# Six row places instead of eight, and one gate weight kept on chip for all latent groups

## The reference, cut to what matters

```python
proj = h @ lp['w_in']
u, v, zb, q, k, rv, rg_f, rg_b, gm = jnp.split(proj, IN_OFFSETS, axis=-1)
y_a = _gmlp_mix(jax.nn.gelu(u), jax.nn.gelu(v), lp['gmlp_ws'], lp['gmlp_b'], lp['gmlp_ln_g'])
y_b = _pool_mix(zb, lp['pool_w'], lp['pool_scale'], grid)
...
ga, gb, gc = jnp.split(jax.nn.sigmoid(gm), N_BRANCH, axis=-1)
merged = ga * y_a + gb * y_b + gc * y_c.astype(x.dtype)
x = x + gt1 * (merged @ lp['w_out'])
...
# _peer, per block of 128 tokens
qp = (xt @ wq).reshape(t, PEER_HEADS, 2, PEER_DKEY // 2)
sc = jnp.einsum('thsk,hsnk->thsn', qp, subkeys).astype(jnp.float32)
top_s, top_i = lax.top_k(sc, PEER_TOPK)
...
act = jax.nn.gelu(jnp.einsum('thkd,td->thk', u_tab[expert], xt).astype(jnp.float32))
wgt = (g * act).astype(xt.dtype)
return jnp.einsum('thk,thkd->td', wgt, v_tab[expert]).astype(xt.dtype)
```

## Time and profile before

| | |
|---|---|
| median of three executions | 4546.5 us (4540.7 to 4548.8) |
| the profiled execution | 4553.9 us, its span 4552.2 us |
| PE busy | 3751.7 us (82%), 12065 instructions |
| DVE busy | 2791.9 us (61%) |
| ACT busy | 1640.3 us (36%) |
| POOL busy | 1626.2 us (36%), 1280 gathers |
| DMA | 1671.7 MB, mean 367 GB/s over the span |
| gathers (queue q0) | 1342.3 MB |

### The profile page before, as it was taken

How to read it: one execution, slowest core, us unless ns; L and a number is a source line. 1 busy time by engine, 2 the same in 40 slices (tenths; PEclk the granted TensorE clock), 3 DMA queues, 4 the chain that set the end, 5 groups by cost and what they waited for, 6 DMA issues and landing times. The chain is left out here.

```text
span 4552.2 us, 44585 instructions
## 1 busy us (share of the span) xinstructions
PE 3751.7 (82%) x12065; PEld 1565.1 (34%) x12065; DVE 2791.9 (61%) x6341; ACT 1640.3 (36%) x5133; POOL 1626.2 (36%) x1312
## 2 busy tenths in 40 slices
PE   8999999999998689999776887888777566666666
PEld 6654455656553233443221222342222111111110
DVE  1122777577676976655898557455678984444444
ACT  4211345232113343334344334334344553333333
POOL 0000123223222333333434434343444445555554
PEclk9999999999999799999876999998887666666666
DMA  8646688789999989999998999999999999999998
GB/s 345 235 161 219 261 331 328 274 305 378 372 405 401 364 352 402 383 380 407 402 393 325 421 415 403 397 396 413 403 402 382 395 395 413 413 421 413 415 422 348
DMA packets 277595, 1671.68 MB, mean 367 GB/s; under 512 B 30496, under 2 KB 47968, under 8 KB 90848
## 3 DMA queue, kind: packets, MB, share of 16 engines
q0 software_dynamic: 184320, 1342.26, 73.6%
q1 hardware_dynamic: 84864, 303.14, 17.3%
q10 hardware_dynamic: 8160, 23.43, 1.6%
HBM read 1630.93 MB, written 37.78 MB: 367 GB/s over the span
## 5 line engine op out<-in xcount | busy, mean ns | idle before, releaser
L1103 POOL DMA_INDIRECT slots<-in_peer,idxR x1280 | 1619.9, 1266 | 2854.9 <-PE ps L1417 1793.8
L1417 PE MATMUL ps<-slots,lhs 128*64 128x512 f32 x4544 | 1496.2, 773 | 698.9 <-ACT lhs L1159 684.8
L1707 DVE CUSTOM_DVE_ANT_0 slots<-slots,h2R 128x1024 f32<-128x1024 f32 x1280 | 1547.3, 1224 | 756.5 <-issue 694.8
L1399 PE MATMUL ps<-ring,arena 128*128 128x512 f32 (+1 forms) x3264 | 1368.8, 576 | 15.4 <-ACT arena L1349 6.9
L1417 PEld LDWEIGHTS ps<-slots,lhs 128*64 128x64 f32 x4544 | 296.8, 159 | 1792.0 <-ACT lhs L1159 1537.7
L1399 PEld LDWEIGHTS ps<-ring,arena 128*128 128x128 f32 x3264 | 624.0, 195 | 771.7 <-issue 754.3
L1148 ACT ACTIVATE gelus<-dots 128x1 f32<-128x1 f32 x1280 | 256.4, 200 | 1511.4 <-DVE dots L1707 1499.6
L1159 ACT ACTIVATE lhs<-fold,wgts 128x64 f32<-128x64 f32 x1136 | 395.1, 348 | 37.2
L1151 ACT ACTIVATE wgts<-gelus,gsmR 128x1 f32<-128x1 f32 x1280 | 377.1, 295 | 42.4 <-ACT gelus L1148 0.5
L1399 PE MATMUL ps<-ring,slots 128*128 128x512 f32 (+1 forms) x576 | 223.3, 548 | 0.0
L1719 DVE SCALAR_TENSOR_TENSOR slots<-slots,wgts 128x1024 f32<-128x1024 f32 x135 | 173.0, 1282 | 79.0 <-ACT wgts L1151 73.0
(11 more groups left out here) (206 smaller groups left out, 2407.0 us busy)
## 6 DMA issues: line engine op xcount, KB each, us to landing
ring<-in_whead SPq DMA_DIRECT2D x48, 1024.0 KB
ring<-in_wa SPq DMA_DIRECT2D x48, 1024.0 KB
ring<-in_wq SPq DMA_DIRECT2D x32, 1024.0 KB
slots<-in_peer,idxR POOLq DMA_INDIRECT x1280
ring<-in_wgc SPq DMA_DIRECT2D x16, 1024.0 KB
ring<-in_wgb SPq DMA_DIRECT2D x16, 1024.0 KB
ring<-in_wout SPq DMA_DIRECT2D x16, 1024.0 KB
o_scratch<-inb SPq DMA_DIRECT2D x80, 128.0 KB
```

Source lines behind the costliest of these rows:

```text
L1103: g.indirect_dma_start(out=slot(R), out_offset=None, in_=a["peer"], in_offset=bass.IndirectOffsetOnAxis(ap=idxR[:, p % KEEP, g2, col:col + ...
L1399: done = mm(out, lhsT, rhs, start=n == 0, stop=n == KD - 1)
L1417: done = mm(ps[j * HALF:(j + 1) * HALF, g2, :], weights, slot(R)[:, D + j * UW:D + (j + 1) * UW], start=start, stop=stop)
L1707: v.tensor_tensor_reduce(out=u, in0=u, in1=h2R[:, g2, :], scale=1.0, scalar=0.0, op0=ALU.mult, op1=ALU.add, accum_out=dots[:, R % LHS:R % ...
```

## The change

`SLOTS` falls from 8 to 6, so every row uses six places and `displaced(R)` is R - 6 throughout; `slots` keeps its size of eight places (`PLACES`). Places 6 and 7 become `kept`, a home for the first unit of the pooled branch's gate. SP loads it once in the latent stage, behind a wait for group 0's indices (`idx_done`), by when the scores in these places have been read. For groups 1 to 3 the gate's tiles of j = 0 read `kept` and belong to no unit, so the ring no longer loads that unit for them. Group 0 loads it into the ring as before.

```diff
-SLOTS = 8
+SLOTS = 6
+PLACES = 8
...
-                ev = self.add("gb", 1, ("wgb", j, k), g=k, i=i, j=j, c=cs[i], p=BASE[k] + i, pe=7.0, act=.7, dve=1.5)
+                ev = self.add("gb", 1, ("wgb", j, k) if j or not k else None, g=k, i=i, j=j, c=cs[i], p=BASE[k] + i, pe=7.0, act=.7, dve=1.5)
...
-        slots = sb("slots", [P, SLOTS, 2 * D])
+        slots = sb("slots", [P, PLACES, 2 * D])
...
+        kept = slots[:, SLOTS:PLACES, :].rearrange("p s n -> p (s n)")
...
                 elif k == "z" and ev.i == 0:
+                    if ev.g and ev.j:
+                        sp.wait_ge(s["idx_done"], 8 * BASE[1])
+                        sp.dma_start(kept, a["wgb"][0]).then_inc(s["kept_in"], 16)
...
-                    if ends and n == KD // 2 - 1 and tile == last[ev.u]:
+                    if ends and n == KD // 2 - 1 and tile == last.get(ev.u):
...
                     room(t)
+                    if k == "gb" and ev.j == 0 and ev.g:
+                        pe.wait_ge(s["kept_in"], 16)
+                        w = kept.rearrange("p (k n) -> p k n", k=KD)
```

More of the change, by code:

```diff
@@ L793, in build @@
         modd = nc.dram_tensor("mod_scratch", [8, D], F32, kind="Internal").ap()
-        names = """const_in silu_done cond_in bmod_in pool_consts decay_in lg_exp lg_u lg_ln lg_done exps_done mask_done
+        names = """const_in silu_done cond_in bmod_in kept_in pool_consts decay_in lg_exp lg_u lg_ln lg_done exps_done mask_done
             m8_out m8_in mod_done pk_done modd_out lng_in subk_in psc_in pw_in hT_out hg_in state_in state_out
```

## The result

The changed kernel takes 4694.1 us (median of four, 4692.9 to 4701.6) against 4544.8 us before: the ratio is 1.0323, 95% interval 1.0311 to 1.0335. It is 149 us slower. The sign was forecast and the wide range, 4532 to 4730, holds the time, but the forecast's own range, 4556 to 4670, does not: the forecast was +65 us, and the loss is more than twice that.

The account below looks back on a forecast made before the run. The bound varies by stretch: TensorE, VectorE while ranking, DMA when full, with the row-place loop as a second budget. Losses of 75 us less 10 gained, +65 on 4546.5, gave 4610 us; own range 4556 to 4670, wide range 4532 to 4730.

Parts of the forecast that it names:

- The tail: From 3700 us on, only rows are left and DMA sets the pace; 5 us lost for pauses at a chunk's end.
- G: Time from POOL's gather instruction to the row's dot product; 7.76 us with a short queue, 12.7 beside weight loads.
- H: Time from a row's dot product to POOL's next instruction for its place; 9.75 us in the dense stretch, 5.05 at the end.
- The stretch from 1300 to 2200: TensorE and DMA both nearly full; six places were to lose 20 us, between 0 and 46.
- The dense stretch: From 2500 to 3500 us, DMA full at 0.99; six places were to lose 35 us, a third of 101.
- midway value: Dense stretch with G = 10.2 us: a row takes 3.33 us, a loss of 101 us.
- The upper end of G: Dense stretch, three gathers sharing DMA with weight loads: G = 12.7 us, a row takes 3.74, a loss of 238 us.
- rival C: Idle TensorE lowers its own clock, from 0.90 towards 0.80 in the dense stretch: +130 to +200 us, chance 0.22.
- 2200 to 2500: VectorE's expert ranking is the bound, as in 3500 to 3700; 10 us lost for both, 0 to 42.
- A: Faster: the gather queue never runs dry with six places and the saved loads count in full; 4532 to 4537 us, chance 0.18.
- B: Nothing measurable: a small loss of 10 to 20 us equals the gain; 4537 to 4556 us, chance 0.12.
- D: SP stalls on its new wait or the kept load comes late, at group 1's gate; 4550 to 4600 us, chance 0.02.

Follow-up runs that it names:

- the pair with few weight bytes: Weight transfers of groups 2 and 3 cut from 1 MB to 128 KB, in the kernel before with eight places and with six: 4492.5 and 4643.0 us.

## Why the prediction was right or wrong

**Right.** The sign, the bytes, the order, and the absence of a cost for SP's wait, TensorE's wait and the kept load (six places alone gave 1.0330, the change 1.0323). The tail: G fell from 15.3 to 9.9 with H at 5 and 2.49 us a row, +4 us where I said 5. The 500 to 800 stretch, six places in both, did not move. The stretch from 1300 to 2200 lost 22 us where I said 20, but partly by luck: VectorE's waits for gathers grew by 63 us there (83 to 146), not by 40, and a third of that reached the time, not half.

**Wrong, by terms.**
- The dense stretch, "a third of 101: 35 us", measured 89, and this is the step that failed. I let H "shrink towards 5.05" when TensorE waits, and so struck out two thirds of the midway value. H did not shrink: over rows 547 to 882 its mean is 8.1 us before and 7.9 after, while G fell from 15.8 to 11.6 (the i-th gather and the i-th dot of the timelines). A place is held while TensorE is in a tile, as the earlier trace rows show with H = 9.75 and a silence of POOL of 7 us. (G + H)/N with measured means is the time of a row whatever the cause, 19.4/6 = 3.24 us, so it explains nothing by itself; the forecast hung on what H and G would become. The upper end of G, weight loads beside the gathers, was the wrong mechanism (the pair with few weight bytes lost the same 150). The midway value without the third, 101, would have been nearer.
- The sum also left the clock at nothing and kept it for rival C; 43 of the 89 us are longer busy time of TensorE at 0.86 instead of 0.90.
- 2200 to 2500: +20, and 3500 to 3700: -1; I had 10 for both together. The loss of the first is in group 2's queries and ranking, the place in its order that answers to the scene above; that its cause is the same was not tested. By rows, 405 to 517 lose 23 us.
- 800 to 1300: +13, I had 5 (upper end 21), and I gave "within 5 us of itself" as a sign. VectorE's waits for gathers grew from 1 to 47 us there.
- The gain, 10 us, measured 4 (1 slower to 8 faster) with eight places.

By stretches, 89 + 22 + 13 + 19 + 4 = 147 net, where the sum had 75 less the gain of 10.

**The rivals.** A (the queue never runs dry) is out: DMA went from 0.99 to 0.93. B is out by the time. Of C, the clock did fall, from 0.90 to 0.86 in the dense stretch, but not below the 0.85 that I gave as its sign, and TensorE's idle share there rose by 3 points, from 18% to 21%, where C supposed 5. C's time, 4680 to 4750, is the one that came, a clock part and a loop part together. Whether the slower clock caused a part of the loss, or filled time in which rows were late anyway, was not tested apart. D is out: six places alone, without the kept load, took as long.

**The Trainium skill's figure.** I had cited "DMA: Bandwidth & Descriptors", Anatomy of one DMA (2.0 us and the bytes over 436 GB/s, an estimated 4.4 us for a gather). The gather at 3487.20, issued 9 us after any other and with DMA idle before it, was used 5.7 us later. That includes POOL's instruction of 0.94 us, so some 4.8 us are left, near the estimate. My remark that 7.76 us was the least seen in the trace before did not look far enough: the gather at 3376.23 there was used 5.88 us later, after a wait of VectorE's. The sum that I drew from the page, a loss shrunk to the gain, did not come, since the length of one gather was not what decided.

**Open.** Rows 568 to 670, which lose 31 us. There TensorE's waits for rows grew by only 3 us, and its busy time by 27, at a granted clock of 0.88 instead of 0.95 (the kernel before, then the changed one; columns as above):

```profile
2567.32:2870.45 303.13, 250.35 (x770) 93.38 (x768) 190.46 (x383) 123.89 (x391) 122.57 (x102) 0.95 1.01 412
...
2626.71:2961.35 334.64, 277.28 (x785) 100.56 (x785) 190.67 (x382) 125.56 (x395) 124.34 (x103) 0.88 0.93 373
```

So this part of the loss lies beside a lower clock, and what lowered it no run shows. No pair shortened those tiles. What is shown by a run is thus that all of the loss comes with the places, and for some 25 us of it by what mechanism; for the rest the mechanism is argued.

## What to carry to other kernels

A buffer between an engine that works in long tiles and one that runs ahead has to hold what the second consumes during the longest tile; here, in the queries of group 3, six places did not and eight did. Average times over a stretch hide that, and the longest idle times show it. Look for it where the refilling queue stands still for a whole tile and for whether the buffer is already empty at the tile's end, not at the refill's bandwidth. And a transfer saved on DMA engines that are 98% busy may be worth far less than its length (here 15 us of transfers gave at most 8): test the saving alone before paying for it.

## What was not expected of the hardware

With half the bytes a gather's mean time from POOL's instruction to its use in the tail was still 6.3 us with six places, although the shortest after which VectorE had waited took 4.15 us and DMA was only 0.83 busy; why is not shown. Pieces of 4 KB also took more of DMA's time for their bytes: 346 GB/s at a share of 0.96, where the whole gathers of 8 KB pieces moved 414 GB/s at 1.01. And 6.3 MB less on engines 98% busy gave about 4 us (1 slower to 8 faster), not 15.
